# The first sixteen modulation blocks taken out of the weight stream, and the low parts of the first weights moved to VectorE

## The chip, the cores and the metric

The kernel runs on one core of one Trainium2 chip. The metric is the device time of one execution in microseconds (us), the median of several runs.

## What is computed

The kernel computes two transformer blocks on 256 tokens of width 1024, in float32. The first has a mixer of retention and differential attention and then a retrieval over 16384 small experts; the second has two feed-forward parts, a gated and a state-space mixer, and a gate at the end. The change touches only the beginning of the first block, which is, cut to what matters:

```python
mod = silu(c) @ w_mod + b_mod                  # 6 x 1024 values; for x, from c
mod_ctx = silu(c_ctx) @ w_mod + b_mod          # for ctx, from c_ctx
h  = rms_norm(x, norm1_g) * (1 + scale) + shift        # shift: values 0 to 1023, scale: 1024 to 2047
hc = rms_norm(ctx, norm1_g) * (1 + scale_c) + shift_c
proj, proj_c = h @ w_in, hc @ w_in             # w_in: 1024 x 3072
```

`w_mod` is cut into 48 blocks of 128 output values, each block 128 x 1024 (512 KB). Blocks 0 to 7 give shift, 8 to 15 give scale; these sixteen are wanted for both `c` and `c_ctx` before the first projection. Blocks 16 to 47 are wanted later and for `c` alone.

## The kernel before

**Weight stream.** Nearly all weights come as chunks of 128 x 2048 values (1 MB, tensor `wall`), each of two halves of 1024. SyncE (SP) issues them in order into the three places of `raw` (line 840); before a place is written again, SP waits until both halves in it have been read (`read`). For a half that goes into matmuls, ScalarE copies it, rounded, to `w_hi` (line 1403), and `raw - w_hi` is written to `w_lo`, by VectorE (line 1843) or, for the halves in `LO_POOL`, by GpSimd (line 2594). TensorE multiplies hi by hi, hi by lo and lo by hi (`mm3`). `w_hi` and `w_lo` have four places each. `REACH[u]` says up to which split half the engines work ahead when they come to half u.

**The front.** `front_steps()` writes the order of the front out by hand, and every engine walks through this list in its own program, doing its own part of each step. Its first forty halves of `wall` are a mixture: 16 modulation blocks and 24 halves of `w_in`. The list begins, one step after the other:

mod 0, 8, 1, 9; diag 0, xturn 0; mod 2; diag 1, cturn 0, gain 0, rows 0; mod 10, 3, 11; xturn 1, cturn 1, gain 1, rows 1; win(0,0); mod 12, 4, 13, 5; xturn 2, cturn 2, gain 2, rows 2; win(0,1); mod 14, 6, 15, 7; xturn 3, cturn 3, gain 3, rows 3; win(0,2); win(0,3), evac 0; win(1,0) and so on.

- `mod n`: blocks 0 to 7 are VectorE's, two passes over 128 x 1024 values, one with `c_ctx` (line 2002) and one with `c` (line 2005), each followed by a read of the accumulator. Blocks 8 to 15 (`MOD_PE`) are TensorE's, 8 matmuls of 2 columns each, out of `raw`.
- `xturn h`, `cturn h`: TensorE transposes and scales two feature blocks of x and of ctx, 8 matmuls of 128 columns each.
- `gain h`: VectorE waits for TensorE's modulation blocks of this quarter (`s_modu`) and makes gain and shift from them, five small operations (lines 1848 and 1855).
- `rows h`: VectorE and ScalarE write the four feature blocks 4h to 4h+3 in hi and lo to `HX` and `HC`. VectorE begins with two scalings (`scaled`, line 1850), for which it waits until `xturn h` is done. ScalarE, after its part, makes `w_hi` of win(0,h).
- `win(p,h)`: a quarter of the projection of column group p. For p = 0 it is 12 matmuls of 512 columns. TensorE waits for `w_lo` and for the lo parts of `rows h`. On the other engines the step means working ahead to `REACH`.
- `evac 0`: ScalarE copies the first result out of PSUM. It stands behind three more `w_hi` copies in ScalarE's program, and win(1,0) on TensorE waits for it.

The low parts of win(0,0) to win(0,3) are in `LO_POOL`, and are GpSimd's. Blocks 16 to 39 are loaded one by one into four places of their own (`mod_raw`, line 836); SP issues 16 to 19 once VectorE has summed block 7.

Of the kernel before, what the change touches and what calls it, by code (L numbers as in the profile page):

```python
# [20 lines left out]
NRAW = 3  # L21
HF = CH // 2
NH = 4
AHEAD = 3
# [57 lines left out]

U_FRONT, U_OUT1, U_QUERY, U_PEER = 0, 40, 48, 64
U_FFN1, U_XBC, U_IN2, U_OUT2, U_FFN2, U_PLEP, U_PLEG, U_END = 320, 386, 398, 422, 438, 504, 506, 514


NU = 36
# [46 lines left out]
GROUPS = [3, 4, 5, 0, 1, 2]  # L136
# [83 lines left out]

FRONT = front_steps()

HALVES = [s for s in FRONT if s[0] == "win" or (s[0] == "mod" and s[1] < NMOD)]
assert len(HALVES) == U_OUT1
HALF_OF = {s: u for u, s in enumerate(HALVES)}

SPLIT = [u for u in range(U_END) if u >= U_OUT1 or HALVES[u][0] == "win"]
ORD = {u: n for n, u in enumerate(SPLIT)}
LO_POOL |= {HALF_OF["win", p, h] for p in (0,) for h in range(4)}

GATE2 = range(40, 48)
MOD_V = [s[1] for s in FRONT if s[0] == "mod" and s[1] not in MOD_PE] + list(GATE2)
# [2 lines left out]
def mod_slot(n):  # L235


    return (n % 4, (n - NMOD) // 4) if n < GATE2[0] else (4, n - GATE2[0])


def gate2_at(n):
# [4 lines left out]
def mod_issue():  # L246


    at, u = {}, 0
    for s in FRONT:  # L250
        if s in HALF_OF:
            u = HALF_OF[s]
        elif s[0] == "mod":
            at[s] = u
    out, chunk = {}, 0
    for n in range(NMOD, GATE2[0]):
        before = HALF_OF["win", 0, 2] if n < NMOD + 4 else at["mod", n - 4]
        chunk = max(chunk, (before + 9) // 2)
        out.setdefault(chunk, []).append(n)
    for n in GATE2:  # L260
        out.setdefault(PEER_V[gate2_at(n)] // 2 + 1, []).append(n)
    return out
# [5 lines left out]
def reach(u):  # L268


    split = sum(1 for w in SPLIT if w < u)
    n = split
    while n < min(split + AHEAD + (u in ORD), len(SPLIT)):
        needed = range(u, 2 * (SPLIT[n] // 2 - NRAW) + 2)
        if any(w < U_OUT1 and HALVES[w][0] == "mod" for w in needed):
            break
        n += 1
    return n


REACH = [reach(u) if u <= U_OUT1 else min(ORD[u] + AHEAD + 1, len(SPLIT)) for u in range(U_END)]


def win_tables():
# [100 lines left out]
def program(nc, wall, keys_d, cols_d, rows_d, bigrows_d, crow_d, wmod_d, dist_d, x_d, ctx_d, pT_d, gws_d, out_d, n_chunks):  # L385
    assert n_chunks * 2 == U_END
    with ExitStack() as es:
# [3 lines left out]
        def sem(name):  # L391
            return es.enter_context(nc.semaphore(name))
# [71 lines left out]
        s_res = sem("s_res")  # L464

        s_sp, s_spa, s_lam, s_lama = sem("s_sp"), sem("s_spa"), sem("s_lam"), sem("s_lama")
        s_rawm = [sem(f"s_rawm{i}") for i in range(5)]

        s_crow, s_c2, s_modu, s_modv, s_mod = sem("s_crow"), sem("s_c2"), sem("s_modu"), sem("s_modv"), sem("s_mod")
# [48 lines left out]
        def landed(u):  # L518
            n = u // 2
            return s_raw[n % NRAW], 16 * (n // NRAW + 1)  # L520
# [10 lines left out]

        def read(u):

            if u in ORD:
                return LOW[u]
            n = HALVES[u][1]
            return (s_modu, MOD_PE.index(n) + 1) if n in MOD_PE else summed(n)

        def summed(n):

            return s_modv, MOD_V.index(n) + 1

        def raw_half(u):
            return raw[:, (u // 2) % NRAW, (u % 2) * HF:(u % 2 + 1) * HF]
# [23 lines left out]
        qTd[0], qTd[1] = a2.get(256), a2.get(256)  # L568
        assert a2.at <= 2048

        crow_ctx, scr, junk = msk[:, 0, :], msk[:, 1, :], msk[:, 2, :]

        def pj(i, a, b):
            if i < 2:
# [224 lines left out]
        def sync_program(e):  # L799
            e.dma_start(cols[:, :], cols_d).then_inc(s_tab, 16)  # L800
            e.dma_start(crow_ctx, crow_d[1024:2048].partition_broadcast(128)).then_inc(s_crow, 16)
            e.dma_start(crow, crow_d[0:1024].partition_broadcast(128)).then_inc(s_crow, 16)
            for n in range(n_chunks):
                if n == 1:
                    e.dma_start(x[:, :, :], x_d.rearrange("(i p) d -> p i d", p=128)).then_inc(s_x, 16)
                if n == 2:
                    e.dma_start(ctx, ctx_d.rearrange("(i p) d -> p i d", p=128)).then_inc(s_ctx, 16)
                if n == 6:
                    e.dma_start(rows[:, :], rows_d.partition_broadcast(128)).then_inc(s_tab, 16)
                if n == 10:  # L810
                    e.wait_ge(s_tab, 32)
                    e.dma_start(dist, dist_d.rearrange("p (a b) -> p a b", a=4)).then_inc(s_tab, 16)
                if n == 11:
                    e.wait_ge(s_c2, 3)
                    e.dma_start(crow_keep.rearrange("(p d) -> p d", p=1), crow[0:1, :]).then_inc(s_ckeep, 16)
                if n == U_QUERY // 2:
                    e.wait_ge(s_pt_, 8)
                    e.dma_start(skeep, keys_d).then_inc(s_keys, 16)
                if n == U_QUERY // 2 + 4:
                    e.wait_ge(s_res, result(N_PEER, 1, 1))  # L820
                    e.dma_start(x_keep, x[:, :, :].rearrange("p i d -> p (i d)")).then_inc(s_xkeep, 16)
                if n == PEER_V[54] // 2:
                    e.wait_ge(*summed(GATE2[7]))
                    e.dma_start(x[:, :, :].rearrange("p i d -> p (i d)"), x_keep).then_inc(s_xback, 16)
                for m in MOD_ISSUE.get(n, []):
                    place, times = mod_slot(m)
                    if m < NMOD + 4:
                        e.wait_ge(*summed(7))
                        e.wait_ge(s_std, 2)
                    elif m == GATE2[0]:  # L830
                        e.wait_ge(s_w, 24)
                        e.wait_ge(s_ckeep, 16)
                        e.dma_start(crow2, crow_keep.partition_broadcast(128)).then_inc(s_rawm[4], 16)
                    else:
                        e.wait_ge(*summed(m - (1 if m in GATE2 else 4)))
                    e.dma_start(mod_raw[place], wmod_d[m - NMOD]).then_inc(s_rawm[place], 16)
                if n >= NRAW:
                    for u in (2 * (n - NRAW), 2 * (n - NRAW) + 1):
                        e.wait_ge(*read(u))
                e.dma_start(raw[:, n % NRAW, :], wall[n]).then_inc(s_raw[n % NRAW], 16)  # L840
                if n in ACTS_OUT:
                    c = ACTS_OUT[n]
                    e.wait_ge(s_gelu, c + 1)
                    if c > KEPT[0]:
                        e.wait_ge(s_ao, kept(c - 1))
                    e.dma_start(act_keep[c - KEPT[0]], act_made(c)).then_inc(s_ao, 16)
                if n in ACTS_IN:
                    c = ACTS_IN[n]
                    e.wait_ge(s_ao, kept(KEPT[-1]))
                    if c > KEPT[0]:  # L850
                        e.wait_ge(s_ai, kept(c - 1))
                    if c >= KEPT[4]:
                        e.wait_ge(s_w, c - 3)
                    e.dma_start(act_of(c), act_keep[c - KEPT[0]]).then_inc(s_ai, 16)
            for i in range(2):
                for hf in range(2):
                    s_ = slice(hf * 512, (hf + 1) * 512)
                    e.wait_ge(s_fin, 2 * i + hf + 1)
                    e.dma_start(out_d[i * 128:(i + 1) * 128, s_], gt[:, i, s_]).then_inc(s_out, 16)
            e.wait_ge(s_out, 64)  # L860


        def tensor_program(e):
# [17 lines left out]
                t.did(ins, s_tr)  # L881

            def mod_block(n):
                u = HALF_OF["mod", n]
                w = raw_half(u).rearrange("p (k n) -> p k n", k=8)
                t.wait_ge(*landed(u))
                t.wait_ge(s_c2, 1)
                quarter, q = n % 8 // 2, MOD_PE.index(n)
                if quarter >= 2:
                    t.wait_ge(s_mod, quarter - 1)  # L890
                for k in range(8):
                    ins = mm(pm[quarter % 2][:, q, :], w[:, k, :], c2v[:, k, :], k == 0, k == 7)
                t.did(ins, s_modu)
# [942 lines left out]
        def vector_program(e):  # L1836
# [150 lines left out]
            def mod_block(n):  # L1987


                c_ = crow  # L1990
                if n >= NMOD:
                    place, times = mod_slot(n)
                    w = mod_raw[place]
                    if n >= GATE2[0]:
                        times, c_ = times + 1, crow2
                    v.wait_ge(s_rawm[place], 16 * times + 16)
                else:
                    u = HALF_OF["mod", n]
                    w = raw_half(u)
                    v.wait_ge(*landed(u))  # L2000
                    v.wait_ge(s_c2, 2)
                    v.did(e.scalar_tensor_tensor(junk, w, 1.0, crow_ctx, MUL, MUL, accum_out=modT[:, n, 1:2]))  # L2002
                    v.wait_ge(s_c2, 3)
                v.settle()
                v.did(e.scalar_tensor_tensor(w, w, 1.0, c_, MUL, MUL, accum_out=modT[:, n, 0:1]), s_modv)  # L2005
# [740 lines left out]
```

## Time and profile before

| | |
|---|---|
| median of 3 runs | 1744.52 us (1743.62 to 1744.93) |
| the profiled execution: its time | 1747.22 us |
| the profiled execution: its span | 1745.5 us |
| TensorE matmuls, share of the span | 94% |
| VectorE | 72% |
| ScalarE | 52% |
| GpSimd | 5% |
| mean granted TensorE clock | 0.979 of full |

A row of a timeline gives start in us, duration in us, engine, line, operation, what is written and read, shapes, and how many instructions in a row are merged; in brackets the idle time before it and what ended that. The granted clock is given in shares of the full 2.4 GHz: 0.5 is 1.2 GHz. Until the first transition of the clock the record reads 1.00, whatever the clock was: there only the durations of matmuls tell.

### The profile page before, as it was taken

To read this page: it belongs to the slowest core of one execution; us is meant where nothing else is said; L and a number is where in the kernel's file an instruction comes from. 1 tells how busy PE (TensorE), PEld (TensorE's weight loads), DVE (VectorE), ACT (ScalarE), POOL (GpSimd) and SP (SyncE) were. 2 spreads that over 40 slices of the span, in tenths; PEclk is the share of its full clock that TensorE was granted. 3 is DMA by queue.
4 is the path that set the end of the run, shared out by engine and by line. 5 is a ranking of instruction groups with operands and counts; after the bars stand their busy time and mean duration, and the time that the engine had idled before them with its cause. 6 is when DMAs were issued, how large, how long until landed. Compare 5 with 4: busy or idle time off the path is not lost.

```text
span 1745.5 us, 28968 instructions
## 1 busy us (share of the span) xinstructions
PE 1649.3 (94%) x11496; PEld 1480.5 (85%) x11496; DVE 1251.7 (72%) x2028; ACT 909.6 (52%) x1192; POOL 84.2 (5%) x50
## 2 busy tenths in 40 slices
PE   6898887999999999999999999999998979999997
PEld 6776667999999888788999999899998768899996
DVE  5886665899988899987666665655557887655556
ACT  4354555555555554554444444544446757544446
POOL 0100002622000000000000000000000000000000
PEclk9898898999999999999999999999999999999999
DMA  6744233346555555556556455454544533554551
GB/s 258 276 169 157 97 112 139 149 161 212 184 185 192 181 191 207 209 209 246 207 215 217 187 218 186 149 204 179 194 173 154 209 129 121 190 202 173 193 188 75
DMA packets 53418, 318.52 MB, mean 182 GB/s; under 512 B 5953, under 2 KB 6113, under 8 KB 19362
## 3 DMA queue, kind: packets, MB, share of 16 engines
q1 hardware_dynamic: 52098, 310.60, 48.8%
q0 software_dynamic: 1184, 6.05, 0.9%
q8 instruction: 91, 1.49, 0.3%
q14 instruction: 45, 0.37, 0.1%
HBM read 307.17 MB, written 9.47 MB: 181 GB/s over the span
## 4 chain that ended last, share of the span: by engine, by line
PE 73%; DVE 17%; ACT 6%; issue 1%; DMA 1%; SPq 0%; DVEq 0%; ACTq 0%
PE pb L867 73%; DVE w_lo L1843 4%; DVE ar L1843 4%; ACT ar L1403 3%; ACT w_hi L1403 2%; DVE ar L1855 1%; DVE ar L2207 1%; DMA raw<-in_wall 1%; DVE ar L2005 1%; DVE ar L2204 1%; ACT L1403 1%; DVE raw L2005 1%; DVE ar L2002 1%; DVE ar L2211 1%; DVE sm L2070 0%
## 5 line engine op out<-in xcount | busy, mean ns | idle before, releaser
L1843 DVE TENSOR_TENSOR w_lo<-raw,w_hi 128x1024 fp32r<-128x1024 f32 x467 | 572.3, 1226 | 254.0 <-ACT w_hi L1403 228.7
L867 PE MATMUL pb<-HX,w_hi 128*128 128x256 f32 x3904 | 717.0, 285 | 13.0 <-DVE w_lo L1843 6.0
L1403 ACT ACTIVATE w_hi<-raw 128x1024 fp32r<-128x1024 f32 x498 | 529.2, 1063 | 308.2 <-PE pb L867 285.3
L867 PEld LDWEIGHTS pb<-HX,w_hi 128*128 128x128 f32 x3904 | 614.9, 193 | 20.1 <-DVE w_lo L1843 5.2
L867 PE MATMUL pb<-HX,w_lo 128*128 128x256 f32 x1952 | 554.2, 284 | 0.0
L867 PE MATMUL pb<-w_hi,HC 128*128 128x512 f32 (+1 forms) x1648 | 526.5, 391 | 4.2 <-DVE HC L1855 3.3
L867 PEld LDWEIGHTS pb<-HX,w_lo 128*128 128x128 f32 x1952 | 376.4, 193 | 0.0
L867 PEld LDWEIGHTS pb<-w_hi,HC 128*128 128x128 f32 x1648 | 309.5, 188 | 68.4 <-DVE HC L1855 2.7
L867 PE MATMUL pb<-w_lo,HC 128*128 128x512 f32 (+1 forms) x824 | 320.4, 389 | 0.0
L1843 DVE TENSOR_TENSOR ar<-ar 128x512 bf16<-128x512 bf16 (+8 forms) x470 | 247.8, 564 | 53.1 <-ACT ar L1403 33.5
L1403 ACT ACTIVATE ar<-pb 128x512 f32<-128x512 f32 (+3 forms) x200 | 112.6, 563 | 256.9 <-PE pb L867 155.0
L867 PE MATMUL pb<-w_hi,HX 128*128 128x512 f32 x512 | 177.6, 414 | 11.5 <-DVE HX L1843 3.3
L867 PEld LDWEIGHTS pb<-w_lo,HC 128*128 128x128 f32 x824 | 155.5, 189 | 29.0
L867 PE MATMUL pb<-ar 128*128 128x64 bf16 (+3 forms) x1960 | 128.4, 224 | 22.5 <-ACT ar L1403 8.3
L867 PEld LDWEIGHTS pb<-ar 128*128 128x128 bf16 (+2 forms) x1960 | 107.0, 121 | 45.4 <-issue 26.1
L867 PEld LDWEIGHTS pb<-w_hi,HX 128*128 128x128 f32 x512 | 101.6, 198 | 38.0 <-issue 7.2
L867 PE MATMUL pb<-w_lo,HX 128*128 128x512 f32 x256 | 103.8, 405 | 0.0
L1403 ACT ACTIVATE HC<-ar 128x512 fp32r<-128x512 f32 x87 | 55.1, 634 | 93.2 <-PE pb L867 51.9
L1843 DVE TENSOR_TENSOR HC<-ar,HC 128x512 fp32r<-128x512 f32 x87 | 60.3, 693 | 44.9 <-ACT HC L1403 41.3
L2594 POOL TENSOR_TENSOR w_lo<-raw,w_hi 128x1024 fp32r<-128x1024 f32 x31 | 76.1, 2454 | 156.6 <-ACT w_hi L1403 116.4
L1403 ACT ACTIVATE ar<-ar 128x512 f32<-128x512 f32 (+6 forms) x85 | 50.4, 593 | 49.1 <-DVE ar L1850 17.1
L867 PEld LDWEIGHTS pb<-w_lo,HX 128*128 128x128 f32 x256 | 50.8, 198 | 9.5
(145 smaller groups left out, 700.6 us busy)
## 6 DMA issues: line engine op xcount, KB each, us to landing
raw<-in_wall SPq DMA_DIRECT2D x257, 1024.0 KB, 4.8
ar<-in_wmod SPq DMA_DIRECT2D x24, 512.0 KB, 3.7
act_keep<-ar SPq DMA_DIRECT2D x28, 256.0 KB, 5.6
ar<-act_keep SPq DMA_DIRECT2D x28, 256.0 KB, 5.0
x<-in_wmod SPq DMA_DIRECT2D x8, 512.0 KB, 5.3
ar<-in_bigrows POOLq DMA_DIRECT2D x2, 1024.0 KB, 5.0
ar<-acs_keep POOLq DMA_DIRECT2D x2, 1024.0 KB, 7.3
ar<-in_crow SPq DMA_DIRECT2D x2, 512.0 KB, 6.5
```

The costliest lines, as they stand in the source:

```text
L867: return e.matmul(o, l, r, start=start, stop=stop, skip_group_check=True)
L1403: a.did(e.activation(out, in_, func, scale=scale, **kw), sig)
L1843: v.did(e.tensor_tensor(out, a_, b_, op), sig)
L1855: v.did(e.scalar_tensor_tensor(out, a_, s_, b_, op0, op1), sig)
L2002: v.did(e.scalar_tensor_tensor(junk, w, 1.0, crow_ctx, MUL, MUL, accum_out=modT[:, n, 1:2]))
L2005: v.did(e.scalar_tensor_tensor(w, w, 1.0, c_, MUL, MUL, accum_out=modT[:, n, 0:1]), s_modv)
L2204: v.did(e.max(vals[:, c_], src))
L2207: v.did(e.max_index(idx[:, c_], vals[:, c_], src))
L2211: v.did(e.match_replace(src, vals[:, c_], src, NEG))
L2594: p.did(e.tensor_tensor(w_lo[:, made % NH, :], raw_half(w), w_hi[:, made % NH, :].bitcast(F32), SUB), s_lop)
```

## The change

- The sixteen blocks leave `wall` and go to the head of `wmod`, in the order in which the list uses them. SP loads them by twos (1 MB) into eight places that lie in tiles which nobody uses yet: (0,8), (1,9), (2,10), (3,11), (12,4), (13,5), (14,6), (15,7). Four semaphores serve the eight pairs, so pairs 4 to 7 wait on SP until pairs 0 to 3 have landed.
- SP's order of loads is now: cols, two rows of c, pair 0, x, pair 1, ctx, pairs 2 and 3, chunk 0 (win(0,0), win(0,1)), pairs 4 and 5, chunk 1 (win(0,2), win(0,3)), pairs 6 and 7, rows, chunk 2, chunk 3. The load of `dist`, into the place of pair 0, waits for mod 0 and mod 8. Blocks 16 to 19 are issued ahead of chunk 4.
- The four halves win(0,0) to win(0,3) leave `LO_POOL`: VectorE makes all low parts of the front. With the new `REACH` it makes win(0,0) and win(0,1) when it comes to the step win(0,0), behind `rows 1` and ahead of mod 4, and win(0,2) and win(0,3) at the step win(0,1), behind `rows 2` and ahead of mod 6.
- The result of the pass that is not kept (`junk`) goes to another place, and the unit numbers of all later weights fall by 16.

```diff
-U_FRONT, U_OUT1, U_QUERY, U_PEER = 0, 40, 48, 64
+U_FRONT, U_OUT1, U_QUERY, U_PEER = 0, 24, 32, 48
...
-HALVES = [s for s in FRONT if s[0] == "win" or (s[0] == "mod" and s[1] < NMOD)]
+HALVES = [s for s in FRONT if s[0] == "win"]
...
+MOD_FIRST = [s[1] for s in FRONT if s[0] == "mod" and s[1] < NMOD]
 ORD = {u: n for n, u in enumerate(SPLIT)}
-LO_POOL |= {HALF_OF["win", p, h] for p in (0,) for h in range(4)}
...
-        before = HALF_OF["win", 0, 2] if n < NMOD + 4 else at["mod", n - 4]
+        before = HALF_OF["win", 0, 0] if n < NMOD + 4 else at["mod", n - 4]
...
+    return [2, 4, 4][u] if u < 3 else min(u + AHEAD + 1, len(SPLIT))
+
+
+REACH = [reach(u) for u in range(U_END)]
...
-        crow_ctx, scr, junk = msk[:, 0, :], msk[:, 1, :], msk[:, 2, :]
+        crow_ctx, scr, junk = msk[:, 0, :], msk[:, 1, :], PT[:, 0, :]
...
+        first_at = [dist.rearrange("p a b -> p (a b)"), yv.rearrange("p i d -> p (i d)"),
+                    kTd.rearrange("p a b -> p (a b)"), pjxf[:, 0:2048], pjxf[:, 2048:4096], pjxf[:, 4096:6144],
+                    pjcf[:, 0:2048], msk[:, 2:4, :].rearrange("p a b -> p (a b)")]
...
+            def first_pair(q):
+                if q >= 4:
+                    e.wait_ge(s_rawm[q - 4], 16)
+                e.dma_start(first_at[q].rearrange("p (b d) -> p b d", b=2),
+                            wmod_d[2 * q:2 * q + 2].rearrange("b p d -> p b d")).then_inc(s_rawm[q % 4], 16)
+
+            first_pair(0)
+            e.dma_start(x[:, :, :], x_d.rearrange("(i p) d -> p i d", p=128)).then_inc(s_x, 16)
+            first_pair(1)
+            e.dma_start(ctx, ctx_d.rearrange("(i p) d -> p i d", p=128)).then_inc(s_ctx, 16)
+            first_pair(2)
+            first_pair(3)
             for n in range(n_chunks):
                 if n == 1:
-                    e.dma_start(x[:, :, :], x_d.rearrange("(i p) d -> p i d", p=128)).then_inc(s_x, 16)
+                    first_pair(4)
+                    first_pair(5)
                 if n == 2:
-                    e.dma_start(ctx, ctx_d.rearrange("(i p) d -> p i d", p=128)).then_inc(s_ctx, 16)
-                if n == 6:
+                    first_pair(6)
+                    first_pair(7)
                     e.dma_start(rows[:, :], rows_d.partition_broadcast(128)).then_inc(s_tab, 16)
-                if n == 10:
+                if n == 4:
                     e.wait_ge(s_tab, 32)
+                    e.wait_ge(s_modu, 1)
+                    e.wait_ge(*summed(0))
                     e.dma_start(dist, dist_d.rearrange("p (a b) -> p a b", a=4)).then_inc(s_tab, 16)
...
             def mod_block(n):
-                u = HALF_OF["mod", n]
-                w = raw_half(u).rearrange("p (k n) -> p k n", k=8)
-                t.wait_ge(*landed(u))
+                w, here = first_block(n)
+                w = w.rearrange("p (k n) -> p k n", k=8)
+                t.wait_ge(*here)
```

## Rows read from the trace of the kernel before

**Rows 1.** The page: the span, and the shares of the chain that ended last.

```profile
span 1745.5 us, 28968 instructions
...
PE 73%; DVE 17%; ACT 6%; issue 1%; DMA 1%; SPq 0%; DVEq 0%; ACTq 0%
```

**Rows 2.** The chain in order of time, 20 to 75 us: start, us, what.

```profile
4.66 17.08 DMA raw<-in_wall
...
32.02 3.27 DVE raw L2005 x2
...
59.78 3.28 DVE raw L2005 x2
...
68.39 1.07 ACT w_hi L1403
...
71.86 0.61 ACT ar L1403
...
72.61 2.42 PE pb L867 x9
```

**Rows 3.** Timeline, when a load of 1 MB is first used: ScalarE and VectorE.

```profile
14.29 1.06 ACT L1403 ACTIVATE ar<-x 128x1024 f32<-128x1024 f32 x1 [3.04 <-DMA x<-in_x]
16.73 1.23 DVE L2002 SCALAR_TENSOR_TENSOR ar<-raw,ar 128x1024 f32<-128x1024 f32 x1 [2.39 <-DMA raw<-in_wall]
...
19.27 1.06 ACT L1403 ACTIVATE ar<-ar 128x1024 f32<-128x1024 f32 x1 [1.04 <-DMA ar<-in_ctx]
```

**Rows 4.** Timeline of GpSimd: the first of its low parts.

```profile
31.62 2.57 POOL L2594 TENSOR_TENSOR w_lo<-raw,w_hi 128x1024 fp32r<-128x1024 f32 x1 [30.72 <-ACT w_hi L1403]
```

**Rows 5.** Timeline of VectorE, 36 to 72 us.

```profile
36.70 1.12 DVE L1850 TENSOR_SCALAR fsc<-pb,sm,modT 128x256 f32<-128x256 f32 x2
...
40.55 0.43 DVE L1843 TENSOR_TENSOR HC<-fsc,HC 128x256 fp32r<-128x256 f32 x1 [0.69 <-ACT HC L1403]
...
48.47 0.49 DVE L1848 TENSOR_SCALAR modT<-modT,cols 128x2 f32<-128x2 f32 x2 [0.52 <-DVE raw L2005]
...
49.77 1.12 DVE L1850 TENSOR_SCALAR fsc<-pb,sm,modT 128x256 f32<-128x256 f32 x2
...
55.23 1.22 DVE L2005 SCALAR_TENSOR_TENSOR raw<-raw,ar 128x1024 f32<-128x1024 f32 x1
...
63.16 0.49 DVE L1848 TENSOR_SCALAR modT<-modT,cols 128x2 f32<-128x2 f32 x2
...
69.48 3.89 DVE L1843 TENSOR_TENSOR w_lo<-raw,w_hi 128x1024 fp32r<-128x1024 f32 x3 [0.74 <-ACT w_hi L1403]
```

**Rows 6.** Timeline of TensorE: modulation blocks (2 columns), turns (128), win(0,0)'s first (512).

```profile
27.16 6.83 PE L867 MATMUL pb<-cols,raw 128*128 128x2 f32 x32
...
33.85 2.05 PE L867 MATMUL pb<-ar,x 128*128 128x128 f32 x8
...
37.26 0.77 PE L867 MATMUL pb<-w_hi,HX 128*128 128x512 f32 x1
...
40.73 3.63 PE L867 MATMUL pb<-cols,raw 128*128 128x2 f32 x32
44.22 1.14 PE L867 MATMUL pb<-ar,x 128*128 128x128 f32 x8
```

**Rows 7.** TensorE by stretches: length, busy (matmuls), granted clock, DMA share, GB/s.

```profile
45.00:46.00 1.00, 1.00 (x10) 0.74 0.91 377
...
48.00:49.00 1.00, 1.00 (x4) 0.55 0.94 352
66.00:72.00 6.00, 5.36 (x12) 0.50 0.99 407
72.00:73.00 1.00, 0.49 (x2) 0.60 1.02 418
73.00:80.00 7.00, 7.00 (x32) 1.00 0.61 252
```

More of the change, by code:

```diff
@@ L81, in bc @@
     return a.broadcast_to(shape)
-U_FRONT, U_OUT1, U_QUERY, U_PEER = 0, 40, 48, 64
-U_FFN1, U_XBC, U_IN2, U_OUT2, U_FFN2, U_PLEP, U_PLEG, U_END = 320, 386, 398, 422, 438, 504, 506, 514
+U_FRONT, U_OUT1, U_QUERY, U_PEER = 0, 24, 32, 48
+U_FFN1, U_XBC, U_IN2, U_OUT2, U_FFN2, U_PLEP, U_PLEG, U_END = 304, 370, 382, 406, 422, 488, 490, 498
 NU = 36
@@ L221 @@
 FRONT = front_steps()
-HALVES = [s for s in FRONT if s[0] == "win" or (s[0] == "mod" and s[1] < NMOD)]
+HALVES = [s for s in FRONT if s[0] == "win"]
 assert len(HALVES) == U_OUT1
 HALF_OF = {s: u for u, s in enumerate(HALVES)}
-SPLIT = [u for u in range(U_END) if u >= U_OUT1 or HALVES[u][0] == "win"]
+SPLIT = list(range(U_END))
+MOD_FIRST = [s[1] for s in FRONT if s[0] == "mod" and s[1] < NMOD]
 ORD = {u: n for n, u in enumerate(SPLIT)}
-LO_POOL |= {HALF_OF["win", p, h] for p in (0,) for h in range(4)}
 GATE2 = range(40, 48)
@@ L235, in mod_slot @@
 def mod_slot(n):
-    return (n % 4, (n - NMOD) // 4) if n < GATE2[0] else (4, n - GATE2[0])
+    return (n % 4, 2 + (n - NMOD) // 4) if n < GATE2[0] else (4, n - GATE2[0])
 def gate2_at(n):
@@ L268, in reach @@
 def reach(u):
[L271 to L281, printed above, removed]
+    return [2, 4, 4][u] if u < 3 else min(u + AHEAD + 1, len(SPLIT))
+REACH = [reach(u) for u in range(U_END)]
 def win_tables():
@@ L532, in read @@
         def read(u):
[L534 to L537, printed above, removed]
+            return LOW[u]
         def summed(n):
@@ L569, in program, with first_block @@
         assert a2.at <= 2048
-        crow_ctx, scr, junk = msk[:, 0, :], msk[:, 1, :], msk[:, 2, :]
+        crow_ctx, scr, junk = msk[:, 0, :], msk[:, 1, :], PT[:, 0, :]
+        pjxf, pjcf = pjx.rearrange("p i d -> p (i d)"), pjc.rearrange("p i d -> p (i d)")
+        first_at = [dist.rearrange("p a b -> p (a b)"), yv.rearrange("p i d -> p (i d)"),
+                    kTd.rearrange("p a b -> p (a b)"), pjxf[:, 0:2048], pjxf[:, 2048:4096], pjxf[:, 4096:6144],
+                    pjcf[:, 0:2048], msk[:, 2:4, :].rearrange("p a b -> p (a b)")]
+        def first_block(n):
+            q = MOD_FIRST.index(n)
+            return first_at[q // 2][:, q % 2 * 1024:q % 2 * 1024 + 1024], (s_rawm[q // 2 % 4], 16 * (q // 8) + 16)
         def pj(i, a, b):
@@ L802, in sync_program @@
             e.dma_start(crow, crow_d[0:1024].partition_broadcast(128)).then_inc(s_crow, 16)
+            def first_pair(q):
[9 more added lines that the diff above has]
+            first_pair(3)
             for n in range(n_chunks):
                 if n == 1:
-                    e.dma_start(x[:, :, :], x_d.rearrange("(i p) d -> p i d", p=128)).then_inc(s_x, 16)
+                    first_pair(4)
+                    first_pair(5)
                 if n == 2:
-                    e.dma_start(ctx, ctx_d.rearrange("(i p) d -> p i d", p=128)).then_inc(s_ctx, 16)
-                if n == 6:
+                    first_pair(6)
+                    first_pair(7)
                     e.dma_start(rows[:, :], rows_d.partition_broadcast(128)).then_inc(s_tab, 16)
-                if n == 10:
+                if n == 4:
                     e.wait_ge(s_tab, 32)
+                    e.wait_ge(s_modu, 1)
+                    e.wait_ge(*summed(0))
                     e.dma_start(dist, dist_d.rearrange("p (a b) -> p a b", a=4)).then_inc(s_tab, 16)
-                if n == 11:
+                if n == 5:
                     e.wait_ge(s_c2, 3)
@@ L828, in sync_program @@
                         e.wait_ge(*summed(7))
+                        e.wait_ge(s_modu, len(MOD_PE))
                         e.wait_ge(s_std, 2)
@@ L835, in sync_program @@
                         e.wait_ge(*summed(m - (1 if m in GATE2 else 4)))
-                    e.dma_start(mod_raw[place], wmod_d[m - NMOD]).then_inc(s_rawm[place], 16)
+                    e.dma_start(mod_raw[place], wmod_d[m]).then_inc(s_rawm[place], 16)
                 if n >= NRAW:
@@ L1997, in mod_block @@
                 else:
-                    u = HALF_OF["mod", n]
-                    w = raw_half(u)
-                    v.wait_ge(*landed(u))
+                    w, here = first_block(n)
+                    v.wait_ge(*here)
                     v.wait_ge(s_c2, 2)
@@ L2676 @@
     wr = a["w_mod"][0].T.reshape(48, 128, HF)
-    front = np.stack([wi[4 * GROUPS[s[1]] + s[2]] if s[0] == "win" else (wm if s[1] in MOD_PE else wr)[s[1]] for s in HALVES])
+    front = np.stack([wi[4 * GROUPS[p] + h] for _, p, h in HALVES])
     front = front.reshape(-1, 2, 128, HF).transpose(0, 2, 1, 3).reshape(-1, 128, CH)
@@ L2736 @@
     arrays = {"wall": wall, "keys": keys, "cols": cols_h, "rows": rows_h, "bigrows": big_h, "crow": np.concatenate([a["c"][0], a["c_ctx"]]),
-              "wmod": wr[NMOD:], "dist": dist,
+              "wmod": np.concatenate([np.stack([(wm if n in MOD_PE else wr)[n] for n in MOD_FIRST]), wr[NMOD:]]), "dist": dist,
               "x": a["x"][0], "ctx": a["ctx"][0], "pT": pT, "gws": gws}
```

## The prediction

> **What bounds the kernel now.** The page first: the profiled span is 1745.5 us, and 73% of the chain that ended last is TensorE [rows 1]. All that the diff touches ends within the first 75 us, so the page's shares say nothing about it; what counts is which chain leads through the front, and whether a shift at its end reaches the kernel's end. The chain in order of time tells both. Up to 21.7 us it is transfers [rows 2]. From there to 68.4 us it is VectorE's (with ScalarE's part of each `rows`): TensorE is hardly in it. Then come three `w_hi` copies on ScalarE, the evacuation at 71.86, and TensorE's win(1,0) at 72.61. Only its first 17 us are DMA (1% of the chain [rows 1]); later no transfer ends a wait in it. So I let a shift of win(1,0) reach the end in full.
>
> Within VectorE's stretch the reader is to see four passes of modulation blocks that take 3.3 us, the first at 32.02 and the last at 59.78 [rows 2], where the same pass takes 1.22 [rows 5]. They lie where GpSimd makes a low part: 31.62 to 34.19 [rows 4]; the stretched pass ends 1.1 us after that, as if it had run once GpSimd was done. Price of GpSimd's four low parts on the chain: 4 x 2.1 = 8.3 us. They sit in block 3 (one), block 5 (one) and block 7 (two).
>
> **Part by part.** I go through the list with the clock of the profiled run.
>
> Loads. Pair 0, x, pair 1, ctx, pair 2 stand where chunk 0, x, chunk 1, ctx, chunk 2 stood. Loads with 4 KB rows against 8 KB rows: x is first used at 14.29, chunk 1 (8 KB rows) 2.44 after that, ctx (4 KB rows) another 2.54 later [rows 3]. The pairs have 4 KB rows: +0.1 each, three before mod 2: **+0.3**. At 2.5 us each, pair 3 lands by 24.6 and chunk 0 by 27.1; ScalarE wants it at 30.5, so 3.4 us of cover. Chunk 1 lands near 35, pair 7 near 40, chunk 2 near 43, each well ahead of its step. The waits of pairs 4 to 7 on SP end when pair 0 to 3 land, while later loads are still queued: nothing. Chunk 4 now stands behind blocks 16 to 19; its first user comes after 75 us: nothing. The extra waits of `dist`: nothing, it is wanted after 130 us.
>
> Mod 3 to `rows 1`. The stretched pass of mod 3 shrinks, -2.05. But the blocks 10 and 11 on TensorE end only at 33.99, and the turns of x behind them at 35.90 [rows 6], both +0.3. `scaled` waits for these turns: it starts at 36.25 instead of 36.70 [rows 5]. Of 2.05 us only **-0.45** is kept; TensorE is next late here.
>
> Low parts 0 and 1. `rows 1` ends at 40.98 - 0.45 = 40.5. Then VectorE makes two low parts, 1.25 each by the three in 3.89 us [rows 5] (their `w_hi` are ready: ScalarE makes the second right behind `rows 1`): +2.5. Mod 5 loses its stretch: -2.1. VectorE reaches gain 2 at 47.9, where gain 2 began at 48.5 before [rows 5].
>
> **The ring.** Here the change adds a wait. TensorE's program is in order: turns of quarter 1, win(0,0), blocks 12 and 13, turns of quarter 2. GpSimd had low part 0 ready at 34.2, and win(0,0) ran straight behind the turns, from 37.26 [rows 6]. Now it waits for VectorE until 40.5 + 1.25 = 41.8, and behind it are queued the 32 matmuls of blocks 12 and 13, for which gain 2 waits, and the turns, for which `scaled` of `rows 2` waits. Before, these were done at 44.4 and 45.4, over 3 us early. What that costs is set by TensorE's clock. A projection matmul takes 0.23 us at 2.4 GHz and 0.43 at 1.2 GHz (12 in 5.4 us at a granted clock of 0.50, 32 in 7.0 at 1.00 [rows 7], less the pipeline's end); 32 modulation matmuls take 3.6 us at the one and 6.8 at the other, eight turns 1.1 and 2.05 [rows 6]. The granted clock fell at 45.5 (the turns before had followed 3.6 us of modulation blocks), rose at 48.9, after 3.7 us of turns and projection, and at 72.8, 6.2 us after the projection that began at 66.6 [rows 7]. TensorE would now stand idle from 37.9 to 41.8 and then begin at 1.2 GHz.
> - Ring A: the clock rises 3.7 to 4 us into win(0,0), the lower bound seen. win(0,0) ends at 46.3. Modulation blocks did not hold the clock before (it fell 6.8 us after the rise at 38.7, matmuls of 0.39 us from there); with less projection behind this rise I let it fall near 49: 24 matmuls in 2.7 us, 8 in 1.7, ending at 50.8; turns until 52.85. `scaled` starts at 52.9 instead of 49.77 [rows 5]: **+3.1**. If the clock stays up: 49.95, 51.1, and gain 2 ends at 51.3: +1.5.
> - Ring B: it does not rise within win(0,0) (5.1 us long, against the 6.2 seen as upper bound). 46.9, 53.8, 55.85: +6.1.
>
> Low parts 2 and 3. Behind `rows 2` VectorE waits for `w_hi`, as it did at 69.48 (0.74 idle [rows 5]), and makes two: +3.25. Blocks 6 and 7 lose two and one stretches in all: -4.15, for mod 7's two passes. Together **-0.9**. Gain 3 (63.16 before [rows 5]) and `rows 3` come at +2.2 (A), +0.6 (A, clock stays up), +5.2 (B). Behind the turns of quarter 2 TensorE has win(0,1), blocks 14 and 15, turns: 5.1 + 6.8 + 2 us at most from 54.7, that is 68.6, against `scaled` at 66.7; more likely, with turns and projection back to back and so a risen clock, 63. I take **+0.4**.
>
> Evacuation. ScalarE's three copies and the evacuation set win(1,0) [rows 2], not win(0,3), which ends at 72.1 before and does not lead now either. But the clock rose at 72.8, just as win(1,0) began. Afterwards TensorE is idle some 3 us ahead of it, and 3.7 us at half speed would cost 1.85. Between 0 and 1.85 I take **+0.9**.
>
> The sum for ring A: 2.2 + 0.4 + 0.9 = **+3.5 us**; the +0.3 is in the times above. Against the profiled time of 1747.22 that is 1750.7; the runs shown have a median 2.7 us lower, so 1744.5 + 3.5 = 1748.0.
>
> A rule of the Trainium skill speaks against the change as well: by its page "TensorE: Matmul & The Clock Gate", section "What's actually happening", "the default state is throttled, and activity releases the throttle". The rows agree (the start, and 66 to 72 us). Taken strictly, a TensorE that has just stood idle would run all of win(0,0) and what follows it at the lower clock, which is ring B; taken loosely, ring A.
>
> **The rivals.**
> 1. Ring B: +5.2 + 0.9, without the delay of win(0,1): **1750.6**. For it: win(0,3) went from 66.6 to 72.1 wholly at half clock. Against: twice the rise came after 3.7 us.
> 2. The relief wins: the clock is up all through, or the ring closes in time. One mechanism: VectorE without GpSimd beside it. win(0,0) 41.8 to 44.6, blocks 12 and 13 to 48.2, gain 2 at 48.2 as VectorE arrives; `scaled` 49.5 (-0.3), then -0.9: **-1.2, 1743.3**. It decides where the blocks 12 and 13 end before 48. It cannot be over 0.2%: 8.3 us of stretches against 5.8 us of low parts and `w_hi` wait, and the 1.6 lost at gain 1. Against it: TensorE was at half speed whenever it had waited.
> 3. Ring A with a clock that stays up, and no clock lost later: +0.6 to +1.5: **1745.5**.
> 4. The loads come late: ten loads now go ahead of chunk 0, before one. If each takes 0.35 us longer than 2.5, chunk 0 is late for ScalarE at 30.5; beyond that each us costs one, so rates a third lower give +6: **1750.5**. Against: five loads in a row kept 2.4 to 2.6 us.
> 5. The change does not do what it says to the chain: another releaser takes the place, within 1 us: **1744.5**.
>
> **How the numbers follow.** A measurement of this kernel can tell about 0.2%, 3.5 us, from no change: below 1741.0 faster, above 1748.0 slower. Ring A 0.42 (its own range +2.2 to +5.5, half of it beyond the bound), ring B 0.26, relief 0.08, clock up 0.12, late loads 0.05, nothing 0.07. Slower: 0.21 + 0.25 + 0.04 = 0.50; faster: 0.03, for a relief later in the front that I don't see; same: 0.47. The range takes in rivals 1 and 3: 1744.0 to 1751.5.
>
> **What would show it.** In the timeline after: no GpSimd low parts, all modulation passes at 1.22 us; VectorE's first `w_lo` at about 40.5; win(0,0) at 41.8 instead of 37.3 behind an idle TensorE released by `w_lo`; VectorE idle ahead of gain 2, released by TensorE, for 1.5 to 6 us; granted clock of 0.5 from the first rise's absence on, somewhere between 42 and 55 us; win(1,0) at 74.5 to 78 instead of 72.6; and from there the same durations to the end. The prediction is wrong if win(0,0) starts before 40, if the first low part comes before `rows 1` ends, if VectorE does not idle ahead of gain 2, or if a shift at 72.6 is not found again at the end of the span.

## The result

| | before | changed |
|---|---|---|
| median | 1744.52 us | 1748.75 us (1747.08 to 1750.47, 11 runs) |
| ratio | | 1.0026, 95% interval 1.0018 to 1.0035 |
| two more series of the changed kernel | 1744.71, 1744.60 | 1749.08 (1.0022, 1.0013 to 1.0031), 1749.43 (1.0028, 1.0017 to 1.0038) |
| span of the profiled execution | 1745.5 us | 1747.0 us, in two more 1745.9 and 1747.3 |

The changed kernel is slower by 4.2 to 4.8 us by the medians, 0.22 to 0.28% by the ratios. The two profiled spans alone would have said 1.5 us. The profiled execution of the kernel before was 2.7 us above its median, that of the changed kernel was its median; and in the latter the front was shorter than in the other profiles of this kernel, as comes below.

**The profile after.** GpSimd has four instructions fewer (46 for 50), and every pass of a modulation block takes 1.22 us. VectorE's groups from 10 to 73 us, with shapes kept apart (count, busy us and mean ns, idle time before and what ended it):

```profile
L2024 DVE SCALAR_TENSOR_TENSOR ar<-ar 128x1024 f32<-128x1024 f32 x8 | 9.8, 1225 | 0.3
L2021 DVE SCALAR_TENSOR_TENSOR ar<-ar 128x1024 f32<-128x1024 f32 x8 | 9.8, 1222 | 14.9 <-DMA ar<-in_wmod 14.9
L1863 DVE TENSOR_TENSOR w_lo<-raw,w_hi 128x1024 fp32r<-128x1024 f32 x7 | 8.6, 1225 | 2.0 <-ACT w_hi L1423 1.5
...
L1868 DVE TENSOR_SCALAR modT<-modT,cols 128x2 f32<-128x2 f32 x8 | 1.8, 228 | 2.9 <-PE pb L887 2.5
```

The last row is what the change put in the place of the stretched passes of [rows 2]: ahead of the gains VectorE now idles, and TensorE is what it waits for. The timeline of VectorE in the same profile:

```profile
20.85 1.23 DVE L2021 SCALAR_TENSOR_TENSOR ar<-ar 128x1024 f32<-128x1024 f32 x1 [1.71 <-DMA ar<-in_wmod]
...
33.11 0.49 DVE L1868 TENSOR_SCALAR modT<-modT,cols 128x2 f32<-128x2 f32 x2 [0.79 <-PE pb L887]
...
35.03 1.12 DVE L1870 TENSOR_SCALAR fsc<-pb,sm,modT 128x256 f32<-128x256 f32 x2 [0.72 <-PE pb L887]
...
39.41 2.56 DVE L1863 TENSOR_TENSOR w_lo<-raw,w_hi 128x1024 fp32r<-128x1024 f32 x2
...
48.55 0.49 DVE L1868 TENSOR_SCALAR modT<-modT,cols 128x2 f32<-128x2 f32 x2 [1.75 <-PE pb L887]
...
62.34 0.49 DVE L1868 TENSOR_SCALAR modT<-modT,cols 128x2 f32<-128x2 f32 x2
```

and TensorE's. It closes the ring: VectorE makes the low part, TensorE then runs win(0,0), blocks 12 and 13 and the turns, and for these VectorE waits.

```profile
34.78 1.91 PE L887 MATMUL pb<-ar 128*128 128x128 f32 x8
40.69 0.80 PE L887 MATMUL pb<-w_hi,HX 128*128 128x512 f32 x1 [4.00 <-DVE w_lo L1863]
...
44.88 3.63 PE L887 MATMUL pb<-cols,ar 128*128 128x2 f32 x32
48.37 1.14 PE L887 MATMUL pb<-ar,x 128*128 128x128 f32 x8
```

win(0,0) starts at 40.69 where it started at 37.26 [rows 6], 4 us after TensorE fell idle, and blocks 12 and 13 end at 48.5, where they ended at 44.4. The first pass of mod 2 begins at 20.8 to 22.1 us in the profiles of all the kernels here, according to when the transfers have landed. So from here on I count from the first pass of mod 2 (21.76 in the kernel before: the end of the transfers in [rows 2]). From there to gain 3 (63.16 [rows 5]) the kernel before takes 41.40 us, this profile 41.49. In two more profiles of the changed kernel the same stretch takes 43.33 and 43.30. VectorE's timeline in the first of these two, and TensorE's:

```profile
50.40 0.49 DVE L1868 TENSOR_SCALAR modT<-modT,cols 128x2 f32<-128x2 f32 x2 [2.98 <-PE pb L887]
52.31 1.13 DVE L1870 TENSOR_SCALAR fsc<-pb,sm,modT 128x256 f32<-128x256 f32 x2 [0.72 <-PE pb L887]
```

```profile
45.76 0.45 PE L887 MATMUL pb<-w_lo,HX 128*128 128x512 f32 x1
46.04 0.40 PE L887 MATMUL pb<-w_hi,HX 128*128 128x512 f32 x1
46.27 4.09 PE L887 MATMUL pb<-cols,ar 128*128 128x2 f32 x32
50.22 2.05 PE L887 MATMUL pb<-ar,x 128*128 128x128 f32 x8
```

In the first profile the clock rose after 2.9 us of win(0,0) and stayed up until 57.2. In this one it rose only after 4.5, two matmuls from the end of win(0,0), and fell again before blocks 12 and 13 were through (their 32 take 4.09 us, the turns 2.05). In the first the wait is 1.75 us, here 2.98 + 0.72.

In the third profile (wait 3.26 + 0.40) the clock did not rise within win(0,0) at all. Its last matmul is still at half speed, and the record has the rise at 47.3, under the modulation blocks:

```profile
46.00 0.63 PE L887 MATMUL pb<-w_hi,HX 128*128 128x512 f32 x1
46.43 4.04 PE L887 MATMUL pb<-cols,ar 128*128 128x2 f32 x32
```

The rise alone does not decide it either. A kernel further down has the same front, with fills ahead of win(1,0) only. There the clock rose 3.0 us into win(0,0) but fell at 47.6, and the wait was 3.02 + 0.72 us:

```profile
45.42 4.82 PE L887 MATMUL pb<-cols,ar 128*128 128x2 f32 x32
```

So what sets the first profile apart is that the clock, once up, stayed up through the blocks and the turns.

Then win(1,0). The chain has one entry of 96 matmuls from win(1,0) on. In the kernel before:

```profile
72.61 22.15 PE pb L867 x96
```

In the three profiles of the changed kernel (one fence each):

```profile
71.78 24.80 PE pb L887 x96
```

```profile
74.24 22.07 PE pb L887 x96
```

```profile
74.05 23.66 PE pb L887 x96
```

The granted clock in the first (length, busy, clock, DMA share, GB/s) says why it takes 2.65 us more:

```profile
70.00:71.00 1.00, 0.00 (x0) 0.94 0.95 393
71.00:77.00 6.00, 5.22 (x12) 0.50 0.62 212
77.00:78.00 1.00, 1.00 (x4) 0.65 0.00 0
```

It fell at 70.9, while TensorE waited for the evacuation, and rose at 77.7, 5.9 us after win(1,0) had begun. In the third it fell only at 74.6, 0.5 us into win(1,0), and rose at 78.0. In the kernel before it rose at 72.8 [rows 7], just as win(1,0) began.

### The profile page after: what moved, and what is told of

The parts are those of the page before. It is cut to its first block, busy times and chain, and to the rows that moved or that the text cites. A ratio compares the mean times of both kernels' runs of the same rounds, so it can differ in the third digit from the quotient of the medians.

```text
span 1747.0 us, 28960 instructions
## 1 busy us (share of the span) xinstructions
PE 1648.5 (94%) x11496; PEld 1480.0 (85%) x11496; DVE 1248.0 (71%) x2032; ACT 908.0 (52%) x1192; POOL 72.9 (4%) x46
## 4 chain that ended last, share of the span: by engine, by line
PE 75%; DVE 16%; ACT 6%; issue 1%; DMA 1%; SPq 0%; DVEq 0%; ACTq 0%
PE pb L887 74%; DVE w_lo L1863 4%; DVE ar L1863 4%; ACT ar L1423 3%; ACT w_hi L1423 2%; DVE ar L1875 2%; DVE ar L2024 1%; DVE ar L2226 1%; DMA ar<-in_wmod 1%; DVE ar L2223 1%; ACT L1423 1%; DVE ar L2230 1%; DVE sm L2089 0%; ACT HX L1423 0%; DVE ar L1868 0%
## 5 line engine op out<-in xcount | busy, mean ns | idle before, releaser
L2613 POOL TENSOR_TENSOR w_lo<-raw,w_hi 128x1024 fp32r<-128x1024 f32 x27 | 64.9, 2402 | 107.5 <-ACT w_hi L1423 66.7
```

Of the source, the lines that this page charges most:

```text
L2613: p.did(e.tensor_tensor(w_lo[:, made % NH, :], raw_half(w), w_hi[:, made % NH, :].bitcast(F32), SUB), s_lop)
```

## The experiments

The kernel before was run beside each of them; its medians were 1744.4 to 1744.7. "Front" is the time from the first pass of mod 2 to gain 3 in the profile.

| kernel | median | ratio, 95% interval | front | 96 entries |
|---|---|---|---|---|
| before | 1744.52 | | 41.40 | 22.15 |
| changed (three series) | 1748.75, 1749.08, 1749.43 | 1.0018 to 1.0035, and as above | 41.49, 43.33, 43.30 | 24.80, 22.07, 23.66 |
| GpSimd's low parts back | 1745.93, 1744.75 | 1.0008 (1.0000 to 1.0017), 1.0001 (0.9991 to 1.0010) | 41.24, 41.25 | 22.02, 22.05 |
| low parts alone moved | 1750.43 | 1.0033 (1.0021 to 1.0046) | 46.10 | 22.04 |
| changed, turns first | 1743.99 | 0.9999 (0.9991 to 1.0008) | 39.84 | 22.04 |
| before, turns first | 1745.47 | 1.0002 (0.9993 to 1.0011) | 41.44 | 22.06 |
| changed, fill before win(0,0) | 1745.78 | 1.0006 (0.9997 to 1.0015) | 40.19 | 22.03 |
| changed, five fills before win(1,0) | 1749.84 | 1.0033 (1.0021 to 1.0045) | 43.38 | (see text) |
| changed, three fills | 1748.24 | 1.0018 (1.0009 to 1.0027) | 43.28 | 22.04 |
| turns first and a warm start | 1743.19, 1742.65 | 0.9990 (0.9981 to 0.9999), 0.9987 (0.9978 to 0.9996) | 38.54, 38.54 | 22.05, 22.06 |

**Which half of the change costs.** First the changed kernel with GpSimd's low parts back.

```diff
 ORD = {u: n for n, u in enumerate(SPLIT)}
+LO_POOL |= {HALF_OF["win", p, h] for p in (0,) for h in range(4)}
```

> The changed kernel with one part undone: GpSimd makes the low parts of win(0,0) to win(0,3) again; the loads by twos stay. Theory A (the ring through VectorE's low parts and the clock of win(1,0) cost the time): GpSimd's passes stretch VectorE's again (3.3 us against 1.22, up to four times), win(0,0) starts at about 36, VectorE does not idle ahead of gain 2, and the time is that of the kernel before within 1.5 us (1743 to 1746). Rival B (the new loads cost it): it stays at 1748 to 1749.

1745.93 us, and no wait for TensorE ahead of gain 1 or gain 2. The stretches are back in its timeline, pass by pass (two rows of four):

```profile
31.31 3.25 DVE L2025 SCALAR_TENSOR_TENSOR ar<-ar 128x1024 f32<-128x1024 f32 x1
...
41.43 3.25 DVE L2025 SCALAR_TENSOR_TENSOR ar<-ar 128x1024 f32<-128x1024 f32 x1
```

The interval touched no change from above, so it was repeated.

> The changed kernel with GpSimd's four low parts again, a second time, to say whether the loads by twos cost anything by themselves (1745.93 against 1744.38 in the first run, with an interval that touches no change). If they do: 1746 and the first pass of mod 2 later than in the kernel before, or the first w_hi copy waiting for its transfer. If they don't: 1744 to 1745, mod 2 at 20.8 to 21.8 and gain 3 41.2 to 41.5 us later, as in the kernel before.

1744.75, ratio 1.0001, and a front of 41.25 us with mod 2 at 21.58. No cost and no gain of the loads by twos is shown: both medians lie within 1.6 us of the kernel before, the second within 0.2.

Then the other half alone, on the kernel before.

```diff
-LO_POOL |= {HALF_OF["win", p, h] for p in (0,) for h in range(4)}
```

> The kernel before with the other part alone: the low parts of win(0,0) to win(0,3) on VectorE, the modulation blocks still in the weight stream. Theory A: it has the ring (win(0,0) waits for VectorE's first low part, VectorE idles ahead of gain 2 for 1.5 to 2 us) and costs +3 to +4 us: 1747.5 to 1749. Rival B (the loads cost it): 1744 to 1745. A third possibility: the stream itself gets in the way, since a place of raw is free only after VectorE has made the low part; then it is above 1750.

1750.43, at the edge of "above 1750". It has the same ring (2.95 + 0.72 us of idle time ahead of gain 2 and `rows 2`) and one more, seen in VectorE's and ScalarE's timelines:

```profile
59.85 2.55 DVE L1842 TENSOR_TENSOR w_lo<-raw,w_hi 128x1024 fp32r<-128x1024 f32 x2 [3.51 <-ACT w_hi L1402]
```

```profile
58.76 2.15 ACT L1402 ACTIVATE w_hi<-raw 128x1024 fp32r<-128x1024 f32 x2 [2.88 <-DMA raw<-in_wall]
```

`w_hi` of win(0,1) and win(0,2) waited 2.88 us for a transfer. The chain of this profile says why it came late:

```profile
41.09 9.03 PE pb L866 x44
50.18 0.33 SPq L839
50.60 8.13 DMA raw<-in_wall
58.76 1.07 ACT w_hi L1402
```

SP could refill the place in `raw` only when TensorE had read the blocks queued behind win(0,0), at 50.18. So the two halves of the change belong together: the loads by twos take away a wait of 2.8 us that the moved low parts would otherwise bring (front 46.10 against 43.3; the medians differ by less, 1750.43 against 1748.75 to 1749.43).

**Cutting the ring.** On TensorE alone, blocks 12 and 13 and the turns behind them go ahead of win(0,0), the next ones ahead of win(0,1).

```diff
+def pe_front():
+
+    steps = list(FRONT)
+    for h in (0, 1):
+        w = ("win", 0, h)
+        steps.remove(w)
+        steps.insert(steps.index(("cturn", h + 2)) + 1, w)
+    return steps
...
-            for name, n, *more in FRONT:
+            for name, n, *more in PE_FRONT:
```

> The changed kernel with another order on TensorE alone: blocks 12 and 13 and the turns of quarter 2 come ahead of win(0,0), blocks 14 and 15 and the turns of quarter 3 ahead of win(0,1). This cuts the ring. Theory A1 (the wait in the ring is what costs): VectorE no longer idles ahead of gain 2 (1.75 us in the profile of the changed kernel), rows 3 come 1.5 to 2 us earlier, and the time falls by that, to about 1747. Theory A2 (the lost clock at win(1,0) costs the most): the time follows the clock there; with win(1,0) at the full clock another 2.7 us less, 1744; with it at half clock 1747.

1743.99: 4.8 us less than the changed kernel. VectorE no longer idles ahead of gain 2:

```profile
33.43 0.49 DVE L1880 TENSOR_SCALAR modT<-modT,cols 128x2 f32<-128x2 f32 x2 [0.78 <-PE pb L899]
...
39.73 2.55 DVE L1875 TENSOR_TENSOR w_lo<-raw,w_hi 128x1024 fp32r<-128x1024 f32 x2
...
47.23 0.49 DVE L1880 TENSOR_SCALAR modT<-modT,cols 128x2 f32<-128x2 f32 x2
...
61.01 0.49 DVE L1880 TENSOR_SCALAR modT<-modT,cols 128x2 f32<-128x2 f32 x2
```

The front is 39.84 us, 1.56 shorter than before the change: the relief from GpSimd, net of four low parts, once nothing takes it back. The expectation had named the wait (1747) and the clock at win(1,0) (1744) as alternatives, and counted the wait by the first profile, 1.75 us. Further profiles below have 3.0 + 0.7 us, and against those the front is 3.5 us shorter; win(1,0) also ran at the full clock here (22.04). The same order on the kernel before is the control.

> The control for the reordering: the kernel before with the same new order on TensorE, blocks 12 and 13 and the turns ahead of win(0,0), 14 and 15 and the turns ahead of win(0,1). There no engine waited for TensorE between mod 3 and win(1,0). Theory: no change, 1743.5 to 1745.5. Rival (the new order is good or bad by itself, by the clock that it leaves to win(1,0) or because the places in the weight stream come free later): more than 2 us away from that.

1745.47, ratio 1.0002, front 41.44: the order is worth nothing where VectorE did not wait for TensorE.

**The clock in the ring.** The order is left and the idle TensorE is given two matmuls of constants, whose result nobody reads, behind the turns of quarter 1.

```diff
+                    if (n, more[0]) == (0, 0):
+                        for _ in range(2):
+                            mm(PB[3][:, :], ident, cols[:, COFF["dtw"][0]:COFF["tri"][1]], True, True)
                     projection(n, more[0])
```

> The changed kernel with two extra matmuls of constants on TensorE behind the turns of quarter 1, where it stands idle for 4 us ahead of win(0,0). Theory (half the price of the ring is the low clock after that idle time): win(0,0) runs at the full clock, blocks 12 and 13 end at 47 or earlier, VectorE idles 0.5 us or less ahead of gain 2 instead of 1.75 to 3.7, and the median falls by 1.3 to 3 us, to 1746 to 1747. Rival (the order alone costs it, whatever the clock): the idle time stays above 1.5 us and the median at 1748 to 1749.

1745.78, 3.3 us less than the changed kernel beside it. Of the idle time 1.41 us are left, win(0,0) begins at the full clock, and blocks 12 and 13 are through in time but for 0.45 us:

```profile
37.19 2.80 PE L887 MATMUL pb<-cols 128*128 128x512 f32 x4
41.39 0.50 PE L887 MATMUL pb<-w_hi,HX 128*128 128x512 f32 x1 [1.41 <-DVE w_lo L1866]
...
44.28 3.63 PE L887 MATMUL pb<-cols,ar 128*128 128x2 f32 x32
```

```profile
47.94 0.49 DVE L1871 TENSOR_SCALAR modT<-modT,cols 128x2 f32<-128x2 f32 x2 [0.45 <-PE pb L887]
```

So of the wait of 1.75 to 3.7 us all but 0.45 was the price of the half clock, and the order alone would have cost little. (The median is still 1.1 us above that of the kernel before beside it; the interval takes in no change. win(1,0) ran at the full clock here too, 22.03, which may be a part of the 3.3 us.) That is the rival of this run refuted, and it says what the ring needs: both, the order and the clock that falls while TensorE waits.

**Is the first profile the rule?** The changed kernel unaltered, twice more.

> The changed kernel unaltered, for a second profile. Its first profile showed VectorE idle ahead of gain 2 for 1.75 us and gain 3 at 41.5 us after the first pass of mod 2; the changed kernel with fillers ahead of win(1,0), whose front is the same, showed 3.02 + 0.72 us and 43.4. Theory (the moment at which TensorE's clock rises within or behind win(0,0) sets the wait, and differs between executions): the wait lies between 1.7 and 3.8 us, and the two terms, gain 3 against mod 2 and the stretch of 96 entries from win(1,0) on (22.1 or 24.8 us), explain the span within 1 us. Rival (the first profile is the rule): 1.75 us again. Median 1748 to 1749.

> The changed kernel unaltered once more, for a third profile of it and a direct comparison with the next run on the same chip. Expected: median 1748 to 1749.5; VectorE idle ahead of gain 2 for 1.7 to 3.8 us; gain 3 at 41.5 to 43.5 us after the first pass of mod 2.

2.98 + 0.72 and 3.26 + 0.40 us of idle time, fronts of 43.33 and 43.30, medians 1749.08 and 1749.43. With the two kernels that fill only ahead of win(1,0), whose front is unaltered (43.38 and 43.28), that makes four profiles near 43.3 and one at 41.49. The first profile is the exception. The second half of the first expectation, that front and 96 entries explain the span within 1 us, fell: the later stretches differ too. From the end of the 96 entries to the end of the span the kernels of the table take between 1646.7 and 1651.1 us, two profiles of one and the same kernel (GpSimd's low parts back) 1650.4 and 1646.7. In these two the granted clock was low there for 55 us in the one and for 46 in the other, so that TensorE's clock takes part in this difference as well.

**The clock at win(1,0).** Five fills between win(0,3) and win(1,0), then three.

```diff
+                    if (n, more[0]) == (1, 0):
+                        for _ in range(5):
+                            mm(PB[7][:, :], ident, cols[:, COFF["dtw"][0]:COFF["tri"][1]], True, True)
                     projection(n, more[0])
```

> The changed kernel with five extra matmuls of 512 columns on TensorE (of constants, into a PSUM bank that is free there), between win(0,3) and win(1,0), where TensorE stood idle for 2.95 us. Theory A2 (win(1,0) begins at half clock after that idle time): the stretch of 96 entries of the chain from win(1,0) on takes 22.2 us instead of 24.8, and the median falls by up to 2.6 us, to 1746 to 1747. Theory A1 (the clock there is chance and as often lost in the kernel before): the median stays at 1748 to 1749.

1749.84, no gain. The clock did stay up, but the fills were too long:

```profile
71.01 4.46 PE L887 MATMUL pb<-cols 128*128 128x512 f32 x10
74.91 0.80 PE L887 MATMUL pb<-w_hi,HX 128*128 128x512 f32 x1
```

Five calls make ten entries of 0.44 us; the evacuation had begun at 73.41 and win(1,0), by the distances of the other profiles, could have started at 74.1. The fills gave back 0.8 us of what they saved.

> Three fillers ahead of win(1,0) instead of five: 2.6 us at the full clock, which fits into the idle time of 1.7 to 3 us better than the 4.5 us of five that delayed win(1,0) by 0.8 us. Theory (a half clock at win(1,0) costs 2.7 us in some executions, one in three profiles so far, so 0.9 on the mean): median 0.5 to 1 us below the changed kernel's on the same chip. Rival (it costs nothing on the median): the same median as the changed kernel.

1748.24, 1.2 us below the changed kernel on the same chip (1749.43), with win(1,0) 9.45 us after gain 3 as in all others and 22.04 us for the 96 entries. The two intervals overlap (1.0009 to 1.0027 and 1.0017 to 1.0038), so that the half clock there costs about 1 us on the median is likely but not shown.

**A version that beats both.** What was left in the front of the reordered kernel were 0.78 and 0.71 us of waiting for TensorE around gain 1, behind blocks 10 and 11 at the half clock. Four fills of 256 columns at 21.3 us, where TensorE waits for the norms of ctx, let the clock rise earlier.

```diff
                 elif name == "cturn":
+                    if n == 0:
+                        for _ in range(4):
+                            mm(PB[3][:, 0:256], ident, cols[:, COFF["dtw"][0]:COFF["iota"][1]], True, True)
                     t.wait_ge(s_ctx, 16)
```

> The changed kernel with the reordering on TensorE (1744.0 in its own run) and four extra matmuls of 256 columns of constants ahead of the first turns of ctx, where TensorE stood idle for 3.07 us at the start. Theory: the clock rises before blocks 10 and 11, which then take 3.6 us instead of 6.8; VectorE no longer idles 0.78 us ahead of gain 1 and 0.71 us ahead of the scalings of rows 1, and the time falls by 1 to 1.5 us, to 1742.5 to 1743. Rival (extra matmuls delay the turns and give nothing): 1744 to 1745.

1743.19, and blocks 10 and 11 take 4.92 us instead of 6.83, the turns of ctx before them 1.13 instead of 2.05:

```profile
21.29 3.34 PE L899 MATMUL pb<-cols 128*128 128x256 f32 x8
24.57 1.13 PE L899 MATMUL pb<-ar 128*128 128x128 f32 x8
25.54 4.92 PE L899 MATMUL pb<-cols,ar 128*128 128x2 f32 x32
```

VectorE waits for TensorE nowhere between mod 3 and gain 3; the front is 38.54 us. Again:

> The reordered and warmed version a second time (1743.19, ratio 0.9990 with an interval of 0.9981 to 0.9999 against the kernel before). If it is really faster than the kernel before: 1742.5 to 1743.8 again, gain 3 at 38.5 us after mod 2. If that was chance: 1744 or above.

1742.65, ratio 0.9987 (0.9978 to 0.9996), the same front of 38.54 us, though the clock took another course: blocks 10 and 11 ran at the full clock, and blocks 12 and 13 behind them at the half.

```profile
25.53 3.63 PE L899 MATMUL pb<-cols,ar 128*128 128x2 f32 x32
31.28 6.83 PE L899 MATMUL pb<-cols,ar 128*128 128x2 f32 x32
```

In this order TensorE is early enough for VectorE with either. Against the kernel before it is 1.5 to 2 us faster, 0.1%, with both intervals below 1; against the changed kernel beside it 5.9 and 6.8 us.

## Why the prediction was right, point by point

1748.0 was forecast, with 1744.0 to 1751.5; 1748.75 was measured, on the side forecast, and just over the bound of 0.2% (1748.0) that had half of the chance; its interval reaches to both sides of that bound.

- *What bounds, and that a shift reaches the end.* Right. win(1,0) comes 9.45 us after gain 3 in all but one of the profiles, and there the fills delayed it. That the shift reaches the end shows in the medians (front 3.5 us shorter with the turns first, median 4.8 us less). Single spans do not show it: "the same durations to the end" did not hold, and win(1,0), expected at 74.5 to 78, came at 71.78, 74.24 and 74.05.
- *GpSimd's price, 8.3 us.* Right: the stretches come and go with its four instructions. Net of the low parts the relief is 1.56 us with the ring cut, and 2.86 (41.40 - 38.54) with the waits around gain 1 gone too. Rival 2 had 1.2.
- *Loads, +0.3.* Not found: the changed kernel's profiles have mod 2 at 20.85, 21.48 and 21.30, those with the stream 21.76, 21.24 and 20.79, a scatter larger than the term. The difference of 0.1 us for 4 KB rows was read from two intervals, which was too few. With GpSimd back no cost of the loads is shown.
- *Mod 3 to rows 1, -0.45 with the late loads in it, -0.75 without.* Right: from mod 2 to the scalings of `rows 1` 14.18 us instead of 14.94 (36.70 [rows 5] less 21.76), and TensorE is what is waited for.
- *The ring.* Right in place, order and size, not in the course of the clock. Forecast from mod 2 on: the scalings of `rows 2` at +2.8 (A), +1.2 (clock stays up). Measured against 28.01 before: 29.01, 30.83 and 30.80, that is +1.0 in one profile and +2.8 in two. The first is what rival 3 had for a clock that stays up. Ring A's detail, a rise inside win(0,0) and a fall before blocks 12 and 13 have ended, is the second profile. The third is ring B by its condition, a clock that does not rise within win(0,0), but not by its price: ring B had all of blocks 12 and 13 at the half clock (6.8 us) and so +5.8; the clock rose 0.8 us into them, they took 4.04, and the price was ring A's.
- *Low parts 2 and 3, -0.9.* Right: 43.33 - 41.40 = 1.93, which is 2.8 - 0.9.
- *win(0,1) delays rows 3, +0.4.* Wrong: in no profile of the changed kernel does VectorE wait for TensorE ahead of gain 3. The turns and win(0,1) ran back to back and the clock was up again for blocks 14 and 15, as the "more likely 63" said; the term should have been nothing.
- *The clock at win(1,0), +0.9 out of 0 to 1.85.* The mechanism was right, the upper end too low: 2.65, 0 and 1.5 us in three profiles. From the start of win(1,0) in the first profile the low clock lasted 5.9 us, not the 3.7 that I had taken from the shortest rise seen.
- *The sum.* The pieces read from the three profiles come to 1.3 us (front) and 1.4 us (win(1,0)) on the mean, 2.7 in all, against 4.2 to 4.8 by the medians. Between 1 and 2 us are not located. The forecast held 0.7 us for late loads and for win(0,1) that were not there; they stand in the sum where the unlocated part is, and so far the nearness of 3.5 to the measured 4.2 is luck. The unlocated part may lie in later stretches, where profiles of the same kernel differ by up to 4 us, or in fronts and clocks at win(1,0) that are longer in other executions than in the three profiled ones; no run here settles it. That the cause is the ring rests on the experiments, not on this sum: with GpSimd's low parts back or with the other order the 4 us are gone, and with the full clock at win(0,0) all but about 1 us of them.

The rivals of late loads and of a change without effect are refuted, by the kernel with GpSimd back and by the intervals. Against the relief the prediction said that TensorE was at half speed whenever it had waited. The kernel before has an exception: win(0,2) began at 58.71 behind 2.72 us of waiting, and the clock fell only at 59.2.

## What to carry to other kernels

Before work is moved from a slow helper engine to the engine that bounds the stage, look what is queued on third engines behind the result: here four low parts on GpSimd, which stretched VectorE's passes by 8.3 us, were replaced by 5.1 us of VectorE's own, and an in-order TensorE that now had to wait for VectorE held back matmuls for which VectorE waits. Reordering the waiting engine's queue, independent work first, gave back all of it. And an idle stretch on TensorE can cost twice, once as a wait and once as half a clock behind it, so when a wait is put ahead of it, price what follows at both clocks, and look at more than one profile.

## What the runs showed of the hardware

- The same program, after the same 4.0 us of idle time, had its clock rise 2.9 us into win(0,0) in one execution, 4.5 us in another, and in a third only 6.1 us after its start. In a fourth profile of the same front it rose after 3.0 us and fell at 47.6. The front was 41.49 us where the clock then stayed up, and 43.3 to 43.4 in the others.
- Modulation matmuls of 2 columns are no sure hold for the clock, nor does it always fall under them. With fills ahead of them blocks 10 and 11 took 4.92 us for 32 in one profile (3.6 at the full clock, 6.8 at the half; it fell at 27.6, under them) and 3.63 in the other, where it fell at 30.5 and the next 32, from 31.28 on, took 6.83 without a rise. In the kernel before blocks 12 to 15 ran at the full clock throughout.
- Two fills of 2.8 us in an idle time of 4.2 us, leaving 1.4 us idle, were enough to begin win(0,0) at the full clock, and made the front 3.1 us shorter. Ahead of win(1,0), without a fill, the clock fell within 2.95 us of idle time in one profile, and behind 2.97 us, 0.5 us into win(1,0), in another. In a third it had fallen at 69.8 under win(0,3), and rose at 73.2, while TensorE was idle.
- A VectorE pass with two operands in SBUF that starts while GpSimd makes a low part takes 3.25 to 3.4 us instead of 1.22, whatever the source of its operands, `raw` or the new places.
